# A hybrid encoder on one core: the output projection written as seven half-size products

## The reference, cut to what matters

```python
m = jax.nn.sigmoid(gate_a) * (a @ w_branch_a[l]) + jax.nn.sigmoid(gate_b) * (b @ w_branch_b[l])
x = x + rms_norm(m @ w_out[l], norm_mix_post[l])
f = conv_ffn(rms_norm(x, norm_ffn_pre[l]), w_up[l], conv_w[l], conv_b[l], w_down[l])
```

## Time and profile before

| | |
|---|---|
| median of 3 runs | 2427.83 us (2427.76 to 2428.31) |
| span of the profiled execution, first to last instruction | 2426.0 us |
| TensorE busy | 2413.1 us, 99% |
| VectorE busy | 1825.9 us, 75% |
| ScalarE busy | 1302.4 us, 54% |
| GpSimd busy | 195.1 us, 8% |
| mean granted TensorE clock | 0.999 |
| branch loop, first layer | 503.6 to 570.2 us |
| output projection, first layer | 570.2 to 638.5 us |
| first eight up parts, first layer | 638.5 to 674.8 us |

### The profile page before, as it was taken

How to read it: one execution, slowest core, us unless ns; L and a number is a source line. 1 busy time by engine, 2 the same in 40 slices (tenths; PEclk the granted TensorE clock), 3 DMA queues, 4 the chain that set the end, 5 groups by cost and what they waited for, 6 DMA issues and landing times.

```text
span 2426.0 us, 40808 instructions
## 1 busy us (share of the span) xinstructions
PE 2413.1 (99%) x16410; PEld 2251.7 (93%) x16410; DVE 1825.9 (75%) x2403; ACT 1302.4 (54%) x2014; POOL 195.1 (8%) x236
## 2 busy tenths in 40 slices
PE   9999999999999999999999999999999999999998
PEld 9999989998999999888899998899989999998887
DVE  6666777754888998978585567777649889999784
ACT  6444666543555556556454456665436555554563
POOL 0001011100200000003110011011002000000031
PEclk9999999999999999999999999999999999999999
DMA  5454444344323233833233544343443232346421
GB/s 179 138 179 135 137 138 146 117 169 150 105 72 100 84 103 108 300 114 130 97 128 125 179 148 133 128 140 126 173 148 109 68 90 84 109 155 252 153 95 61
DMA packets 290411, 321.52 MB, mean 133 GB/s; under 512 B 10416, under 2 KB 223920, under 8 KB 290224
## 3 DMA queue, kind: packets, MB, share of 16 engines
q1 hardware_dynamic: 215744, 171.39, 22.7%
q10 hardware_dynamic: 74480, 147.53, 16.8%
HBM read 253.60 MB, written 65.27 MB: 131 GB/s over the span
## 4 chain that ended last, share of the span: by engine, by line
PE 96%; ACT 2%; issue 1%; DVE 1%; POOL 0%; ACTq 0%; DVEq 0%; POOLq 0%
PE ps L863 23%; PE ps L1143 14%; PE ps L1325 13%; PE ps L1088 9%; PE ps L836 6%; PE ps L1431 5%; PE ps L1071 5%; PE ps L1294 3%; PE ps L1261 3%; PE ps L850 3%; PE ps L1041 2%; PE ps L915 1%; PE ps L1411 1%; PE ps L1060 1%; PE ps L972 1%
## 5 line engine op out<-in xcount | busy, mean ns | idle before, releaser
L2048 DVE TENSOR_TENSOR wlo<-raw,whi 128x1024 fp32r<-128x1024 f32 (+1 forms) x152 | 163.9, 1079 | 54.8 <-ACT whi L3018 54.8
L863 PE MATMUL ps<-hT_hi,whi 128*128 128x384 f32 x608 | 203.1, 334 | 0.0
L863 PE MATMUL ps<-hT_hi,wlo 128*128 128x384 f32 x608 | 203.1, 334 | 0.0
L863 PE MATMUL ps<-hT_lo,whi 128*128 128x384 f32 x608 | 203.1, 334 | 0.0
L3032 ACT ACTIVATE U<-ps 128x384 f32<-128x384 f32 x152 | 74.8, 492 | 223.2 <-PE ps L863 223.2
L1325 PE MATMUL ps<-whi,PH_hi 128*128 128x512 f32 x456 | 179.0, 393 | 0.0
L1325 PE MATMUL ps<-whi,PH_lo 128*128 128x512 f32 x456 | 177.6, 390 | 0.0
L1325 PE MATMUL ps<-wlo,PH_hi 128*128 128x512 f32 x456 | 177.5, 389 | 0.0
L1509 DVE TENSOR_TENSOR wlo<-raw,whi 128x2048 fp32r<-128x2048 f32 x53 | 121.9, 2301 | 69.2 <-ACT whi L2368 69.2
L1637 DVE TENSOR_TENSOR wlo<-raw,whi 128x1024 fp32r<-128x1024 f32 (+1 forms) x98 | 102.8, 1069 | 79.3 <-ACT whi L2536 79.3
L863 PE MATMUL ps<-S_hi,whi 128*128 128x384 f32 x456 | 152.3, 334 | 0.0
(11 more groups left out here) (333 smaller groups left out, 6999.6 us busy)
## 6 DMA issues: line engine op xcount, KB each, us to landing
raw<-w_up_dram SPq DMA_DIRECT2D x88, 512.0 KB
raw<-w_in_dram SPq DMA_DIRECT2D x64, 512.0 KB
raw<-w_down_dram SPq DMA_DIRECT2D x60, 512.0 KB, 4.7
raw<-w_in_dram SPq DMA_DIRECT2D x16, 1024.0 KB
zT<-gst ACTq DMA_DIRECT2D x40, 384.0 KB, 2.4
GT<-zT ACTq DMA_DIRECT2D x16, 768.0 KB, 5.9
pD<-CG ACTq DMA_DIRECT2D x26, 384.0 KB, 2.3
zT<-hn ACTq DMA_DIRECT2D x48, 192.0 KB, 1.9
```

The source lines that it names most:

```text
L863: ins = mm(ps[:, 4 * (j % 2) + bank, 0:TH], quarter(L, W[y], j, (w,))[:, 0, k * P:(k + 1) * P], sum_operand(a, x, k), start=(opens and k = ...
L2048: v.tensor_tensor(lo, x, hi.bitcast(F32), ALU.subtract)\
```

## The change

`w_out` and `m` are cut in halves both ways: A11, A12 are the first and second half of the features for the first three token tiles, A21, A22 for the last three, B11 to B22 the quarters of `w_out`. Seven products of 3 token tiles x 4 k x 3 passes x 512 columns take the place of eight: P2 = A12 B21, P1 = A11 B11, P5 = S1 T1, P6 = S2 T2, P3 = S4 B22, P7 = S3 T3 (S3 = A11 - A21, which the branch loop leaves in A21's place in `mT`) and P4 = A22 N4, in that order. The sums S1, S2, S4 of activations are made in the branch loop (`r`, `s`, `p` on VectorE, `cr` on ScalarE) in the new tiles R1, R2, R4; T1, T2, T3 and N4 are made from the quarters of `w_out` by VectorE (`out_weight_sum`), in `raw` slot 1 and in tiles EA and EB that lie in `X`. B12 and B22 are loaded there by SyncE, and the residual rows `X` are now loaded by SyncE as EA and EB fall free. Products collect in banks 0 to 5: ScalarE copies out a bank before the next product adds to it (`s2`, `s5`, `u2`), VectorE adds the copies to later banks (`c11`, `c12`, `c22`). The squares of both halves now come from C11, C12, C22 and the last banks. P3 and P6, and P4 and P7, are taken token tile by token tile, in turns. Eight units are counted where there were four, two of them loaded as units.

The core of the diff:

```diff
+WO_PRODUCTS = ("P2", "P1", "P5", "P6", "P3", "P7", "P4")
+WO_TILES = [(n, t) for n in ("P2", "P1", "P5") for t in range(HT)] + [("P6", 0), ("P6", 1), ("P3", 0), ("P6", 2), ("P3", 1), ("P3", 2),
+                                                                     ("P7", 0), ("P7", 1), ("P4", 0), ("P7", 2), ("P4", 1), ("P4", 2)]
...
-        JK = put("JK", [P, 512], F32, m_end - 2048)[0]
+        JK = put("JK", [P, 512], F32, gst1_off)[0]
...
+                sp.wait_ge(ab_dve.sem, ab_dve.at(L, f"l{KD - 1}"))
+                for i, (dst, k0) in enumerate(((EA, 0), (EB, 4))):
+                    sp.dma_start(dst.rearrange("p (k n) -> p k n", n=512), rows(w_out, L, k0, 4, 512, 512)).then_inc(wo_ld[i], 16)
+                sp.wait_ge(s_out, L * 192 + 16)
+                residual_rows(L, 0)
+                load(unit(L, U_WO), [rows(w_out, L, 4, 4, 0, 512)])
+                load(unit(L, U_WO + 1), [rows(w_out, L, 0, 4, 0, 512)])
...
+                sp.wait_ge(wo_sum.sem, wo_sum.at(L, "N4"))
+                load(unit(L, U_UP), up_rows(0), held=wo_product(L, "P1"))
+                sp.wait_ge(w_lo, wo_product(L, "P3")[0] + (1 + CREDIT))
+                residual_rows(L, 1)
+                load(unit(L, U_UP + 1), up_rows(1), held=wo_product(L, "P7"))
+                sp.wait_ge(w_lo, unit(L, U_WO + 7)[0] + (1 + CREDIT))
+                residual_rows(L, 2)
...
+                unit_ready(unit(L, U_WO))
+                pe.wait_ge(br_dve.sem, br_at(L, 6, "tb"))
+                for k in range(4):
+                    pe.wait_ge(br_dve.sem, br_at(L, 4 + k, "ml"))
+                    for t in range(HT):
+                        ins = out_chunk("P2", t, k)
...
+                for what, n in (*WO_TILES[HT:-5], (TURN, 0), ("P7", 1), ("P4", 0), (TURN, 1), ("P7", 2), ("P4", 1), (TURN, 2), ("P4", 2),
+                                (UP, 0), (TURN, 3), (UP, 1), (TURN, 4), (UP, 2), (TURN, 5), *((UP, n) for n in range(3, 8))):
...
+                            if i == 0:
+                                v.tensor_tensor(R1[:, q, :], BT1[:, TH:T], BT2[:, TH:T], ALU.add).then_inc(*br_dve.step(f"r{q}"))
+                                v.tensor_tensor(BT1[:, 0:TH], BT1[:, 0:TH], BT2[:, 0:TH], ALU.add).then_inc(*br_dve.step(f"m{q}"))
+                                done(br_dve, L, f"m{q}")
+                                v.tensor_tensor(BT1[:, TH:T], BT1[:, 0:TH], R1[:, q, :], ALU.subtract).then_inc(*br_dve.step(f"s{q}"))
+                            else:
+                                v.tensor_tensor(BT1[:], BT1[:], BT2[:], ALU.add).then_inc(*br_dve.step(f"m{q}"))
+                                done(br_dve, L, f"m{q}")
+                                v.tensor_tensor(R1[:, q - 4, :], R1[:, q - 4, :], BT1[:, TH:T], ALU.add).then_inc(*br_dve.step(f"r{q}"))
...
+                out_weight_sum("T1")
                 low(unit(L, U_WO + 1))
+                out_sum_low("S1", R1)
+                out_weight_low("P5", EA)
+                out_weight_sum("T2")
+                out_sum_low("S2", R2)
+                for t in range(HT):
+                    out_sum("c11", t)
+                out_weight_low("P6", EA)
+                out_weight_sum("T3")
+                out_weight_sum("N4")
+                out_sum_low("S4", R4)
+                out_weight_low("P3", EB)
                 dve.wait_ge(s_wr, L * 80 + 48)
...
+                def row_sums(s):
+
+                    for name, t in ((("c12", 0), ("c12", 1)), (("c12", 2),), (("c22", 0),), (("c22", 1), ("c22", 2)))[s] if s < 4 else ():
+                        if (name, t) == ("c12", 1):
+                            out_weight_low("P7", raw[:, 1, :])
+                        if (name, t) == ("c22", 0):
+                            last_weight_low()
+                        out_sum(name, t)
...
+                    if t < HT:
+                        done(wo_dve, L, "S4" if t == 0 else f"c11_{t}")
+                        src = C11[:, t, :]
...
                 high(unit(L, U_WO + 1))
...
+                act.wait_ge(br_dve.sem, br_at(L, KD - 1, "p"))
+                out_sum_high("S1", R1)
+                for t in range(HT):
+                    out_copy("s2", t)
+                done(wo_sum, L, "T1")
+                out_weight_high("P5", EA)
+                out_sum_high("S2", R2)
+                out_sum_high("S4", R4)
+                done(wo_sum, L, "T2")
+                out_weight_high("P6", EA)
+                done(wo_dve, L, "S2")
+                row(wrows[:, 0, :], n_ffn_pre, L, s_wr)
+                row(wrows[:, 1, :], n_mix_post, L, s_wr)
+                for t in range(HT):
+                    out_square(t)
+                for t in range(HT):
+                    out_copy("s5", t)
+                act.wait_ge(wo_ld[1], L * 16 + 16)
+                out_weight_high("P3", EB)
+                out_copy("u2", 0)
+                out_copy("u2", 1)
```

More of the change, by code:

```diff
@@ L68 @@
 U_WO = 28
-U_UP = 32
-U_DN = 54
+U_UP = U_WO + 8
+U_DN = U_UP + NFF
 N_DN = 42
@@ L784, in _, with up_rows @@
                         load(unit(L, U_BR + u, i), [rows(w, L, 0, 4, i * 512 + u * 256, 256) for w in (w_a, w_b)])
[L785 to L789, removed]
+                sp.wait_ge(ab_dve.sem, ab_dve.at(L, f"l{KD - 1}"))
[5 more added lines that the diff above has]
+                load(unit(L, U_WO + 1), [rows(w_out, L, 0, 4, 0, 512)])
+                def up_rows(j):
+                    return [rows(w_up, L, 0, KD, j * P + half, P) for half in (0, FF)]
+                sp.wait_ge(wo_sum.sem, wo_sum.at(L, "N4"))
[5 more added lines that the diff above has]
+                residual_rows(L, 2)
+                for j in range(2, NFF):
+                    load(unit(L, U_UP + j), up_rows(j))
                 for r in range(PIECES):
@@ new lines, in out_chunk @@
+                def out_chunk(name, t, k):
+                    bank, opens = (t if name in ("P2", "P5", "P3") else HT + t), name in ("P2", "P1", "P5")
+                    for q, (a, b) in enumerate(PASSES):
+                        ins = mm(ps[:, bank, :], out_operand(name, a, k, t), W[b][:, wo_product(L, name)[3], k * 512:(k + 1) * 512],
+                                 start=(opens and k == 0 and q == 0), stop=(k == 3 and q == 2), skip_group_check=not opens)
+                    return ins
@@ L1518, in low_halves, with norm_stage @@
                 v.tensor_tensor(unit_half(wlo, g, 1), unit_half(raw, s, 1), unit_half(whi, g, 1).bitcast(F32), ALU.subtract).then_inc(w_lo, 1)
-            def norm_stage(c, it, x, residual=None, bank_ready=None, extra=None, between=None, sums=None):
+            def norm_stage(c, it, x, before, extra=None, between=None, sums=None):
                 def split(h):
@@ L1535, in norm_stage @@
                         split(h)
-                    if r < NT and residual is not None:
-                        bank_ready(r)
+                    before(s)
+                    if r < NT:
                         done(c["pool"], it, f"ry{r}")
@@ L1918, in _ @@
-                for t in range(NT):
-                    done(wo_act, L, f"sq{t}")
-                    v.tensor_copy(Y0w[:, t, :], ps[:, t, :]).then_inc(*wo_dve.step(f"y{t}"))
-                low(unit(L, U_WO + 3))
-                dve.wait_ge(s_wr, L * 80 + 48)
-                done(wo_dve, L, f"y{NT - 1}")
-                for n in range(3):
-                    dve.wait_ge(s_x[n], L * 16 + 16)
+                                    .then_inc(*br_dve.step(f"{name}{q}"))
+                            done(br_dve, L, f"tb{q}")
@@ new lines, in out_sum_low, with out_sum @@
+                def out_sum_low(name, src):
+                    done(wo_act, L, name)
+                    hi, lo = WSUM[name]
+                    v.tensor_tensor(lo[:], src[:], hi[:].bitcast(F32), ALU.subtract).then_inc(*wo_dve.step(name))
+                def out_sum(name, t):
+                    n, c, bank, dst = {"c11": ("P1", "s2", HT + t, C11), "c12": ("P3", "u2", t, C12), "c22": ("P7", "s5", HT + t, C22)}[name]
+                    dve.wait_ge(*wo_tile_done(L, n, t))
+                    done(wo_act, L, f"{c}_{t}")
+                    v.tensor_tensor(dst[:, t, :], ps[:, bank, :], dst[:, t, :], ALU.add).then_inc(*wo_dve.step(f"{name}_{t}"))
@@ L1928, in turned_sums @@
                         sum_turned(L, name, t)
[L1930 removed]
+                norm_stage(nr, L, X, row_sums, lambda s: low(unit(L, U_UP)) if s == 3 else None,
                            lambda s: low(unit(L, U_UP + 1)) if s == 5 else None, turned_sums)
@@ L2895, in f @@
                         if s == 3:
-                            high(unit(L, U_UP))
+                            high(unit(L, U_UP), free=wo_product(L, "P7"))
                     return f
```

250 lines of the change are left out of this document (154 added, 96 removed).

## The result

The changed kernel took 2456.77 us, the median of 4 runs (2455.32 to 2458.7), beside 2427.8 for the kernel before on the same chip (2427.65 to 2428.31): a ratio of 1.0119, 95% interval 1.0105 to 1.0134. It is slower, as forecast, but 10.8 us above the predicted 2446 and 3.8 above the end of the range.

The account below looks back on a forecast made before the run. TensorE, busy 99% of the span, was taken as the bound. Per layer 15.3 us of waits against 8.15 saved is 7.2 worse: 2427.8 + 2 x 7.2 + 4 (clock) = 2446 us, range 2436 to 2453.

Parts of the forecast that it names:

- What goes: TensorE's output projection: 252 matmuls a layer instead of 288, saving 8.15 us a layer, 16.3 us in all, if nothing waits.
- What comes, on VectorE: Extra weight sums, low parts and bank adds in the changed stretch: 22 us more VectorE work a layer.
- rival D: VectorE's sums and low parts of 1536 and 2048 go at half the time, making the kernel faster; chance 0.06.
- Wait 2: TensorE stalls 5.4 us a layer before P3, whose weights are late behind ScalarE's squares, which wait for S4.
- rival C: The stall before P3 is absent because ScalarE's squares are early enough: 2431 us; chance 0.09.
- wait 3: TensorE stalls 4.3 us a layer before the first transposes, waiting for hn0 from VectorE's work on the rows.
- Waits 4, the rest: Smaller stalls from the later transposes to the end of the eight up parts: 5.4 us a layer, taken as 3.6.
- The clock: TensorE's clock falls to 1.2 GHz after long waits, 2.6 us each; one and a half payments, 4 us, taken.
- A: Rival: the same TensorE waits, but the clock stays up: 2442 us; chance 0.25.
- B: Rival: the clock falls in the waits before P3 and the first transposes, in both layers: 2452 us; chance 0.08.
- wait 1: TensorE stalls 2.0 us a layer before P1, whose low weight part stands behind T1 in VectorE's queue.
- Edits at nothing: Branch-loop sums, residual rows moved to SyncE's queue, weight loads, new slots and addresses: priced at no time.

Follow-up runs that it names:

- e2_squares: The changed kernel with ScalarE's s5 copies, P3's high part and one u2 copy put ahead of the three squares: 2440.93 us, ratio 1.0054.
- e1_fill: The changed kernel with 60 extra matmuls a layer whose result nobody reads, placed in the three large TensorE waits: 2447.35 us, ratio 1.0081.
- e7_whole: The changed kernel with P6, P3, P7 and P4 each taken whole instead of alternating token tile by token tile: 2439.87 us, ratio 1.005.
- e5_all: The changed kernel with T1 made in the branch loop, squares behind P3's high part, and first transposes behind P7's second tile: 2428.27 us, ratio 1.0002.
- e8b_all_fill: e5_all with 26 short unread matmuls a layer, 12 ahead of the first transposes and 14 ahead of the third: 2426.82 us, ratio 0.9995.
- e3_t1_early: The changed kernel with the sum T1 made in the branch loop, no longer ahead of P1's low part: 2450.67 us, ratio 1.0093.

## Why the prediction was right in its sign and short in its size

**What goes** is right: 36 matmuls a layer, and TensorE's pace at full clock is the 0.227 us it had the earlier trace rows.

**What comes, on VectorE** is right. Sums of 2048 took 2.29 to 2.30 us (predicted 2.28), low parts of 1536 took 1.68 in the chain (1.67). So the lower bound of 1.1 for a sum is excluded, and rival D with it. VectorE's 23.5 us more in a layer's stretch (93.7 less 70.2) answer to the 22 of the sum.

**Waits 1, 2 and 3** were put at 2.0, 5.4 and 4.3 us; they are 2.04, 5.09 and 4.75. Wait 2's cause, the squares in ScalarE's queue with their wait for S4, is shown by e2_squares, and rival C fell with it. Wait 3 is 0.45 longer. The prediction let `hn` of row 0 follow VectorE's work on row 1 without a gap. In the kernel after, VectorE had done that work at 626.98 and stood idle for 0.44 us, until GpSimd's `rsx` was there. GpSimd's operation on one element, in order of time, in a stretch in which VectorE is at rest and then this one, beside VectorE's add `X<-X,TMP`:

```profile
615.12 0.57 POOL L2440 TENSOR_TENSOR rsy<-msy,half_neg 128x1 f32<-128x1 f32 x1
...
625.85 1.53 POOL L2431 TENSOR_TENSOR rsx<-msx,half_neg 128x1 f32<-128x1 f32 x1
```

**Waits 4, the rest**, taken as 3.6, make 15.35 - 2.04 - 5.09 - 4.75 = 3.5. The idle time of a layer is 15.35 us where the sum had 15.3. In part that is luck. The two larger waits of the bookkeeping stand in the trace (TURN 2 1.84 for 1.9, the first up part 0.82 for 1.0), the others were overstated (TURN 3 0.43 for 0.9, the third up part 0.39 for 1.3, TURN 1 nothing for 0.3). Taking off the 1.8 us by which the bookkeeping erred in the kernel before happened to be right in the sum.

**The clock** is the step that failed. The mechanism was right, and its price of 2.6 us a payment not far off (measured 1.6 to 2.9, mean 2.3), but I took one and a half payments and there were five: 11.7 us for 4. That is 7.7 of the 10.8 us that the sum was short. Two choices made it small. I let wait 3 pay in half the cases because it was barely longer than the 4.0 us of the earlier trace rows, and never asked whether a wait of 2 us could pay. The earlier trace rows show one fall, at the end of one idle stretch, and so no smallest wait. And the two rivals beside it shared the same assumption: A had no payment, B had four; none had wait 1. B (2452) was nearest. e1_fill shows the term by itself: with the clock held, the time is 2447.35, 9.4 us less. (The price from the earlier trace rows is 5.28 less 2.6, nearer 2.7 than the 2.6 that I wrote; it changes nothing here.)

**What the sum left out.** 2 x (15.35 - 8.15) + 11.7 is 26.1 of 28.8. The 1.4 us a layer that remain can be read off the matmuls at wait 1, TensorE in order of time:

```profile
578.01 0.39 PE L1314 MATMUL ps<-whi,mT_lo 128*128 128x512 f32 x1
580.44 0.50 PE L1314 MATMUL ps<-whi,mT_hi 128*128 128x512 f32 x1 [2.04 <-DVE wlo L1587]
580.77 0.40 PE L1314 MATMUL ps<-wlo,mT_hi 128*128 128x512 f32 x1
```

Back to back, the second would have started 0.227 after 578.01; it came 2.43 after, so 2.20 us are lost where the view counts 2.04, from the modelled end of a 0.39 record. Then the next starts 0.33 behind it for 0.227. Each wait hides 0.16 us, and the pace right behind it costs a little more. Seven waits a layer (14 in the list above) at 0.16 are 1.1 of the 1.4. It also fits e7_whole, which has ten a layer and no payment: its stretch is 5.3 us longer than before, 11.2 - 8.15 gives 3.1, ten times 0.16 is 1.6, and 0.6 are left for the pace behind them. No run took this by itself; it is argued from the rows.

**Edits at nothing** cost nothing that the trace shows: no wait for a residual row or a weight load appears among TensorE's, and the branch loop ends where it did (570.04 for 570.23).

**Why the gain does not come back.** With everything put right that the runs found, TensorE is idle for 5.7 us in e5_all (103.96 less 98.22 in the first layer) and the clock falls twice in the second layer, of 8.15 us saved. Most of the idle time that is left is waits for `hn`. As I read the order, which no run tests, the row chain of VectorE, ScalarE and GpSimd now has to fit under the last 2.7 us tiles, beside six c adds and two low parts that were not there before. Whether another order of VectorE's list would beat the kernel before stays open; no such order was tried.

## What to carry to other kernels

A form that trades TensorE's work for an engine that is two thirds busy has to be counted as waits, not as a sum of work: 8.15 us saved, and 23.5 us of VectorE's put into a stretch of 104, became 15.35 us of idle TensorE, although VectorE was not full. Find the waits by running each queue in order with row prices, which came within 0.5 us for each wait, and look at what work nobody waits for stands ahead of what TensorE needs. Then give every such wait a possible fall of the clock, down to the 2 us at which it fell here, and the forecast a case in which all of them pay: 30.7 us of waits cost 11.7 us of clock on top. And when an engine waits in the middle of its queue, look at what stands behind: 2.4 us of squares, which waited for S4, held up P3's weights by more than their own length.

## What the runs showed of the hardware that I had not expected

**A short wait pays sometimes.** Waits of 2.03 to 2.4 us can be compared, each in one profiled execution. The clock stayed at 2.4 GHz behind wait 1 of the kernel after in the first layer (2.04), behind TURN 0 of e5_all in the first (2.04), and behind all of e7_whole's (up to 2.4). It fell behind wait 1 of the kernel after in the second layer (2.04), behind the waits before TURN 0 and TURN 2 in the second layer of e5_all (2.03 and 2.11), and behind wait 1 of e2_squares in both layers. Neither the length nor the layer decides: up to wait 1 of the first layer e2_squares is the same program as the kernel after. No wait under 2.03 us in these stretches was followed by a fall. The Trainium skill (TensorE: Matmul & The Clock Gate, What's actually happening) says that the gate's windows run free of the kernel. The trace agrees in that two equal waits end differently; what is counted in a window no run here shows.

**The spread of the runs may go with it.** The kernel after spreads over 3.4 us and e5_all over 3.4; e8b_all_fill, e5_all with 26 unused matmuls a layer, over 0.6 in 11 runs, and the kernel before over 0.9 in 15. That the falls make the spread is not shown: e1_fill, at a clock of 0.999 to 1.000, spreads over 1.5 us in 4 runs, and e3_t1_early, at 0.994 to 0.995, over no more than 1.7.

**A tiny operation is not always tiny beside VectorE.** GpSimd's operation on one element a partition took 0.57 us with VectorE at rest. Beside adds and subtractions of VectorE it took 1.44, 1.53 and 1.39 (622.79, 625.85 and 630.01 in the kernel after); the 1.53 stands on the chain that releases `hn`. Beside others it kept its pace: 0.55 at 661.84, while VectorE made `hT_lo` from `ps`. Which of VectorE's operations lengthen it, no run here settles.
